# The masks of the causal heads' first bank and of half the banded blocks: from matrix products to VectorE, in a hybrid attention trunk

## The chip, the cores and the metric

The kernel runs on one core of a Trainium2 chip. A core has engines that run their own instruction streams and meet through semaphores: TensorE (PE, matrix products into PSUM banks of 128 x 512 f32), VectorE (DVE), ScalarE (ACT), GpSimd (POOL) and SyncE (SP), which here issues the transfers. The metric is the device time in microseconds. Three runs of the kernel before took 1720.56 to 1721.05 us, median 1720.91.

## The reference

Two layers, 512 tokens, width 1024. Each layer mixes three attention branches by gates and then has a squared-ReLU MLP. The change touches the masks of two of the branches:

```python
# branch A, 8 heads, causal, in blocks of 128 queries
s = jnp.where(key_pos[None, :] <= q_pos[:, None], s, -jnp.inf)
p = jax.nn.softmax(s, axis=-1).astype(v.dtype)
# branch B, 8 heads, sliding window of 128, so a block sees itself and the one before it
valid = (diff >= 0) & (diff < SWA_WINDOW)
s = jnp.where(valid[None, :, None, None], s, -jnp.inf)
m = jnp.maximum(jnp.max(s, axis=-1, keepdims=True), sink)
p = jnp.exp(s - m)
p = (p / (jnp.sum(p, axis=-1, keepdims=True) + jnp.exp(sink - m))).astype(v.dtype)
```

Branch C (stick-breaking, 8 heads) has a strict causal mask, which the kernel already applies behind its exponential; it is not touched.

## The kernel before

All matrix work is done in split precision: an operand is stored as a high part (fp32r, made by ACT as a copy) and a low part (the difference, made by DVE), and each product is three products: high by high, high by low, low by high. Weights come in chunks through a ring of four buffers; `split(c)` on ACT and on DVE makes the two parts of chunk c. Scores are kept transposed, keys on the partitions and queries along the columns, so that a softmax's maximum over keys goes across partitions.

A head of branch A (`CAUSAL`) has four key blocks, with 512, 384, 256 and 128 columns of queries that may see them, in three banks: bank 0 holds key block 0 (512 columns, its first 128 the diagonal block), bank 1 key blocks 1 and 3, bank 2 key block 2. A head of branch B (`BANDED`) has three key blocks of 256 columns (own block and next) and one of 128, in two banks; banded heads come in pairs. A mask is a matrix product: the identity by a constant that is -1e30 where the score is to go (`causal_mask`, and in `band_scores`). One head then goes through this chain:

- PE: `scores` (or `band_scores` for a pair), which adds the masks.
- DVE: `biggest`, four steps that fold the blocks into `mx` (512 columns). The first step of a causal head is a copy of bank 0; the first two of a banded head take the maximum with the sink (`floor`).
- GpSimd: the reduction of `mx` across partitions.
- PE: `less_biggest`, which subtracts it (`mla_shift`, `band_shift`).
- ACT: `soft_exp`, the exponential of each bank into `s_f` (1280 columns) or `bs_f` (896).
- ACT: `soft_hi`, the high part `p_hi`. DVE: `probs_lo`, the low part `p_lo`.
- PE: `values`. ACT: `soft_out`, 1/denominator through a logarithm and an exponential. DVE: `soft_out`, the product `of`, which frees the bank of the values.

Each engine's order is written out by hand. In the causal stage DVE's iteration h does: the maximum of head h+1, `mla_q` and `mla_qk` (splits of queries and keys for head h+2), `soft_out(h)`, a weight split, in the first layer's iterations 0 to 3 a part of the rotary angles (`angle_turns`, `angle_less`, `angle`, `angle_ahead`), `probs_lo(h+1)`, and the product of a gate tile (`scaled`), which frees the tile's bank. Projection tiles alternate between two banks, so each waits for the tile two before it. PE's iteration h does: scores of head h+1, `mla_q(h+2)` (with the keys for even heads), values of head h, and a gate tile with `mla_shift(h+1)` in its middle. In the banded stage DVE's iteration t, for the pair 2t and 2t+1, does two maxima, `mixed`, `soft_out`, `band_lo(2t)`, weight splits, `mixed`, `rope_turn` and `rope_in` or `stick_scaled`, then `band_den(2t)`, `band_lo(2t+1)`, `soft_out(2t)`. PE's does `band_values(2t-1)`, `out_tile` and `band_shift` twice, a tile, `band_values(2t)` and `band_scores(t+1)`. In the last pair `stick_scores(0)` follows `band_values(6)`, and waits for the last exponential of the banded heads. `soft_hi` of the odd head waits for the values of the even one.

## Time and profile before

| | |
|---|---|
| median of three runs | 1720.91 us |
| the profiled execution | 1720.57 us, span 1718.8 us |
| PE busy | 1693.2 us, 99% of the span |
| weight loads of PE | 1429.0 us, 83% |
| DVE busy | 1117.5 us, 65% |
| ACT busy | 852.8 us, 50% |
| GpSimd busy | 150.8 us, 9% |
| mean granted TensorE clock | 0.998 |
| chain that ended last | PE 83%, issue 6%, DVE 5%, ACT 3% |

Busy times are those of one profiled execution. Products overlap on PE, so a product's duration in the profile (0.39 us for 512 columns) is longer than the distance from its start to the start of the next; only distances between starts say what a product costs. An idle time of an engine stands in brackets in the timelines, with what released it; it costs only where something on the path waits for that engine. Times in the timelines are from the start of the span. The first layer's causal stage runs from about 51 to 154 us, its banded stage from about 160 to 244; in the second layer they lie some 850 us later.

### The profile page before, as it was taken

The numbers are of one execution on the slowest core, as the hardware profiler recorded it, in microseconds if no ns is written. First come the engines' busy times: TensorE is split into PE (matmuls) and PEld (weight loads), VectorE is DVE, ScalarE is ACT, GpSimd is POOL, SyncE is SP. The second block draws the span as 40 slices with busy tenths as digits, with TensorE's granted clock in tenths as the row PEclk, the third lists the DMA queues.
The fourth block names the chain that finished last, engine by engine and source line by source line (L and its number), as shares of the span: only waits on it lengthen the run. The fifth ranks groups of instructions, "written<-read, shape, count | busy, mean of one in ns | idle before, by whom it ended". The sixth has DMA issues, their size and how long they took to land.

```text
span 1718.8 us, 21730 instructions
## 1 busy us (share of the span) xinstructions
PE 1693.2 (99%) x8533; PEld 1429.0 (83%) x8533; DVE 1117.5 (65%) x1530; ACT 852.8 (50%) x1204; POOL 150.8 (9%) x142
## 2 busy tenths in 40 slices
PE   8999999999999999999999999999999999999997
PEld 6888888888898888888888888888888988888886
DVE  8887888886566534364597777888754765344545
ACT  7576566665455424131466755666644553231223
POOL 0111211111100000000001111111111000000000
PEclk9999999999999999999999999999999999999999
DMA  4121122222332222222321211122224222222222
GB/s 151 66 71 60 62 69 75 78 74 86 135 111 85 93 94 97 99 98 98 120 83 65 77 62 62 62 74 74 74 92 161 78 90 96 98 98 98 98 98 74
DMA packets 47495, 152.02 MB, mean 88 GB/s; under 512 B 5153, under 2 KB 9633, under 8 KB 47394
## 3 DMA queue, kind: packets, MB, share of 16 engines
q1 hardware_dynamic: 45664, 147.36, 24.7%
q10 hardware_dynamic: 1730, 3.28, 0.5%
q8 instruction: 68, 1.11, 0.3%
q14 instruction: 33, 0.27, 0.0%
HBM read 146.42 MB, written 4.19 MB: 88 GB/s over the span
## 4 chain that ended last, share of the span: by engine, by line
PE 83%; issue 6%; DVE 5%; ACT 3%; POOL 1%; DMA 1%; SPq 0%; DVEq 0%; POOLq 0%; ACTq 0%
PE bank L599 78%; PE bank L604 2%; PE bank L856 1%; PE bank L901 1%; POOL mix L2342 1%; ACT w_hi L1053 1%; DVE w_lo L1600 1%; POOL fb L2372 1%; PE bank L703 0%; DMA x<-in_x 0%; DVE hf L1647 0%; ACT dn L1110 0%; ACT dn L1108 0%; DVE h_lo L1635 0%; DVE of L1722 0%
## 5 line engine op out<-in xcount | busy, mean ns | idle before, releaser
L599 PE MATMUL bank<-h_hi,w_hi 128*128 128x512 f32 (+1 forms) x1224 | 477.3, 390 | 6.4 <-DVEq L1739 2.8
L599 PE MATMUL bank<-h_hi,w_lo 128*128 128x512 f32 (+1 forms) x1224 | 471.9, 386 | 0.0
L599 PE MATMUL bank<-h_lo,w_hi 128*128 128x512 f32 (+1 forms) x1224 | 471.6, 385 | 0.0
L1053 ACT ACTIVATE w_hi<-raw 128x1024 fp32r<-128x1024 f32 (+2 forms) x269 | 270.5, 1013 | 206.4 <-DMA raw<-in_w 205.9
L1600 DVE TENSOR_TENSOR w_lo<-raw,w_hi 128x1024 fp32r<-128x1024 f32 (+2 forms) x269 | 316.3, 1179 | 59.5 <-ACT w_hi L1053 52.7
L599 PEld LDWEIGHTS bank<-h_hi,w_hi 128*128 128x128 f32 x1224 | 230.1, 188 | 55.5 <-issue 6.2
L599 PEld LDWEIGHTS bank<-h_hi,w_lo 128*128 128x128 f32 x1224 | 229.9, 188 | 47.1
L599 PEld LDWEIGHTS bank<-h_lo,w_hi 128*128 128x128 f32 x1224 | 230.2, 188 | 44.8 <-issue 1.2
L599 PE MATMUL bank<-u_hi,w_hi 128*128 128x512 f32 (+1 forms) x560 | 208.0, 371 | 0.0
L599 PE MATMUL bank<-u_hi,w_lo 128*128 128x512 f32 (+1 forms) x560 | 207.7, 371 | 0.0
L599 PE MATMUL bank<-u_lo,w_hi 128*128 128x512 f32 (+1 forms) x560 | 207.7, 371 | 0.0
L599 PEld LDWEIGHTS bank<-u_hi,w_hi 128*128 128x128 f32 x560 | 105.5, 188 | 18.3
L599 PEld LDWEIGHTS bank<-u_lo,w_hi 128*128 128x128 f32 x560 | 105.5, 188 | 18.2
L599 PEld LDWEIGHTS bank<-u_hi,w_lo 128*128 128x128 f32 x560 | 105.5, 188 | 18.0
L1934 DVE TENSOR_TENSOR usq<-relu 128x512 f32<-128x512 f32 x64 | 44.2, 691 | 101.7 <-ACT relu L1258 101.2
L1258 ACT ACTIVATE relu<-bank 128x512 f32<-128x512 f32 x48 | 28.6, 595 | 136.5 <-PE bank L599 136.5
L1952 DVE TENSOR_TENSOR y<-bank,y 128x512 f32<-128x512 f32 x32 | 22.1, 691 | 98.7 <-PE bank L599 98.7
L599 PE MATMUL bank<-o_hi,w_hi 128*128 128x512 f32 x192 | 76.6, 399 | 0.0
L1260 ACT ACTIVATE u_hi<-relu 128x512 fp32r<-128x512 f32 x64 | 40.5, 633 | 70.1 <-DVE relu L1929 68.6
L599 PE MATMUL bank<-o_hi,w_lo 128*128 128x512 f32 x192 | 75.0, 390 | 0.0
L2342 POOL TENSOR_TENSOR mix<-mix,gate 128x512 f32<-128x512 f32 x32 | 44.4, 1390 | 346.5 <-DVE gate L1909 346.5
L599 PE MATMUL bank<-o_lo,w_hi 128*128 128x512 f32 x192 | 74.8, 390 | 0.0
(267 smaller groups left out, 2738.7 us busy)
## 6 DMA issues: line engine op xcount, KB each, us to landing
raw<-in_w SPq DMA_DIRECT2D x251, 512.0 KB, 3.2
x<-in_x SPq DMA_DIRECT2D x16, 256.0 KB, 3.5
side_raw<-in_w SPq DMA_DIRECT2D x6, 512.0 KB, 4.9
x_spill<-x ACTq DMA_DIRECT2D x8, 256.0 KB, 2.2
x<-x_spill SPq DMA_DIRECT2D x8, 256.0 KB, 3.0
out_y<-x SPq DMA_DIRECT2D x8, 256.0 KB, 2.1
raw<-in_w SPq DMA_DIRECT2D x8, 192.0 KB, 2.4
raw<-in_w SPq DMA_DIRECT2D x8, 128.0 KB, 2.3
```

The lines of the kernel that those rows point to most:

```text
L599: mm = pe.matmul(o, s, m, start=start and i == 0 and j == 0, stop=last and i == n - 1 and j == 2, skip_group_check=True)
L604: return pe.matmul(o, stationary, moving, start=False, stop=True, skip_group_check=True)
L856: return pe.matmul(to[:, off + col:off + col + w], a, m, start=(r, n, i) in STICK_STARTS, stop=i == 2, skip_group_check=True)
L901: mm = pe.matmul(pv_bank[:, q0:q0 + w], v[:, j, h % 2, :], part[:, s], start=i == 0 and part is p_hi, stop=part is p_lo, skip_group_check= ...
L1053: act.activation(chunk_in(gc, w_hi, side_hi)[:, 0:w], chunk_in(gc, raw, side_raw)[:, 0:w], ACT.Copy)\
L1258: act.activation(relu[:, n % 2, :], tile_bank(name)[:, :], ACT.Relu).then_inc(free_of(name), 1)
L1260: act.activation(u_hi[g % 2][:, t, :], relu[:, n % 2, :], ACT.Square).then_inc(u_h.sem, 1)
L1600: dve.tensor_tensor(chunk_in(gc, w_lo, side_lo)[:, 0:w], chunk_in(gc, raw, side_raw)[:, 0:w], chunk_in(gc, w_hi, side_hi)[:, 0:w].bitcast( ...
L1934: dve.tensor_tensor(usq[:, n % 2, :], relu[:, n % 2, :], relu[:, n % 2, :], ALU.mult)\
L1952: ins = dve.tensor_tensor(y[:, t, :], tile_bank(name)[:, :], y[:, t, :], ALU.add)
L2342: pool.tensor_tensor(mix[:, t, :], mix[:, t, :], gated_at(b, t), ALU.add).then_inc(mix_add.sem, 1)
L2372: pool.tensor_tensor(to, to, tri01[:, :], ALU.mult).then_inc(z_mask.sem, 1)
```

## The change

Constants gain two matrices, `BOUND`: 2^127 where a probability is kept and 0 where it is masked, for the diagonal and for the previous block. ACT copies them into a buffer `bound` in the setup.

Causal heads: bank 0 gets no mask product any more; banks 1 and 2 keep theirs. The first step of the maximum is now a sum of the first 128 columns and the mask constant, and a copy of the other 384. Behind the exponential DVE takes, in place, the minimum of `s_f`'s first 128 columns and `bound`.

Banded heads: in the first bank only the second half is masked by a product (256 columns instead of 512), in the second bank only the last 128 columns (the product of 256 goes). The first two steps of the maximum become (score max sink) + mask in one instruction. Behind the exponential DVE takes the minimum of two blocks of 256 columns and `bound`.

`soft_hi` on ACT waits for the new minimum (`probs_masked`).

```diff
@@ scores (PE)
-                        three(to[:, off + col:off + col + w], [(keys(j), queries(q0, w))], start=off + col == 0)
+                        mm = three(to[:, off + col:off + col + w], [(keys(j), queries(q0, w))], start=off + col == 0)
                         if n + 1 == len(pieces) or pieces[n + 1][3] != b:
-                            causal_mask(to, off, b, MASK_CAUSAL).then_inc(score_full.sem, 1)
+                            if b:
+                                mm = causal_mask(to, off, b, MASK_CAUSAL)
+                            mm.then_inc(score_full.sem, 1)
@@ band_scores (PE)
                                 if b == 0:
-                                    mm = add(band[r][0][:, :].rearrange("p (a c) -> p a c", a=2), cst[:, IDENT, :],
-                                             both.unsqueeze(1).broadcast_to([P, 2, 2 * P]))
+                                    mm = add(band[r][0][:, 2 * P:4 * P], cst[:, IDENT, :], both)
                                 else:
-                                    add(band[r][1][:, 0:2 * P], cst[:, IDENT, :], both)
                                     mm = add(band[r][1][:, 2 * P:3 * P], cst[:, IDENT, :], cst[:, MASK_CAUSAL, :])
@@ soft_hi (ACT)
                     act.wait_ge(*p_exp(banks_of(n + 1)))
+                    act.wait_ge(*p_mask(n + 1))
@@ setup (ACT)
+                act.activation(bound[:, :], cst_f[:, BOUND * P:(BOUND + 2) * P], ACT.Copy).then_inc(const_set, 1)
@@ biggest (DVE)
                         if banded and i < 2:
-                            ins = dve.tensor_scalar(to[:, q0:q0 + w], src, floor, None, ALU.max)
+                            both = cst[:, MASK_CAUSAL:MASK_PREV + 1, :].rearrange("p a c -> p (a c)").bitcast(F32)
+                            ins = dve.scalar_tensor_tensor(out=to[:, q0:q0 + w], in0=src, scalar=floor, in1=both,
+                                                           op0=ALU.max, op1=ALU.add)
                         elif i == 0:
-                            ins = dve.tensor_copy(to[:, q0:q0 + w], src)
+                            dve.wait_ge(const_set, 1)
+                            dve.tensor_tensor(to[:, 0:P], src[:, 0:P], cst[:, MASK_CAUSAL, :].bitcast(F32), ALU.add)
+                            ins = dve.tensor_copy(to[:, P:SEQ], src[:, P:SEQ])
@@ new (DVE)
+                def causal_masked(h):
+                    dve.wait_ge(const_set, 4)
+                    dve.wait_ge(*p_exp(banks_of(h) + 1))
+                    dve.tensor_tensor(s_f[:, 0:P], s_f[:, 0:P], bound[:, 0:P], ALU.min).then_inc(p_mask.sem, 1)
+
+                def band_masked(n):
+                    dve.wait_ge(*p_exp(banks_of(HEADS + n + 1)))
+                    halves = bs_f[n % 2][:, 0:6 * P].rearrange("p (a c) -> p a c", a=3)[:, 0:3:2, :]
+                    dve.tensor_tensor(halves, halves, bound[:, :].unsqueeze(1).broadcast_to([P, 2, 2 * P]), ALU.min)\
+                       .then_inc(p_mask.sem, 1)
@@ order of DVE
                     for j in range(NB - 1):
                         mla_v(j)
+                    causal_masked(0)
                     split(C["gate", 0, 2] + 2)
@@ in the loop over causal heads, behind the angles
                         if h + 1 < HEADS:
+                            causal_masked(h + 1)
                             probs_lo(h + 1, s_f[:, :], p_hi[:, :], p_lo[:, :])
@@ in the loop over banded pairs
                             soft_out(HEADS + n - 1)
+                        band_masked(n)
                         band_lo(n)
...
                             stick_scaled(0, t - 1)
+                        band_masked(n + 1)
                         band_den(n)
                         band_lo(n + 1)
```

DVE's order in the first layer's causal stage, from the split of head 3's queries to head 4's maximum (`tt` are the angles, `mix` the gate). Before:

```order
L1600 TENSOR_TENSOR w_lo<-raw,w_hi 128x1024
L1578 SCALAR_TENSOR_TENSOR tt_151<-tt_152,tt_151 128x512 x2
L1582 TENSOR_SCALAR tab<-tt_151 128x512
L1690 TENSOR_TENSOR p_lo<-s_f,p_hi 128x1280
L1682 TENSOR_TENSOR mix<-bank,rstd_x 128x512
L1711 CAST mx<-bank 128x512
L1713 TENSOR_TENSOR mx<-bank,mx 128x384
```

And with the change:

```order
L1604 TENSOR_TENSOR w_lo<-raw,w_hi 128x1024
L1582 SCALAR_TENSOR_TENSOR tt_152<-tt_153,tt_152 128x512 x2
L1586 TENSOR_SCALAR tab<-tt_152 128x512
L1727 TENSOR_TENSOR s_f<-s_f,bound 128x128
L1694 TENSOR_TENSOR p_lo<-s_f,p_hi 128x1280
L1686 TENSOR_TENSOR mix<-bank,rstd_x 128x512
L1718 TENSOR_TENSOR mx<-bank,cst 128x128
L1719 CAST mx<-bank 128x384
L1721 TENSOR_TENSOR mx<-bank,mx 128x384
```

The minimum stands behind the angles and ahead of the low part, and the copy is in two. PE's order at the end of `band_scores`, the second bank (masks are `bank<-cst`, key block 3's scores `128x128`), and the first product of `band_values`. Before:

```order
L828 MATMUL bank<-wq_hi,wk_hi 128x128 x2
L828 MATMUL bank<-wq_lo,wk_hi 128x128 x2
L828 MATMUL bank<-wq_hi,wk_lo 128x128 x2
L604 MATMUL bank<-cst 128x256
L604 MATMUL bank<-cst 128x128
L604 MATMUL bank<-cst 128x256
L604 MATMUL bank<-cst 128x128
L599 MATMUL bank<-bp_hi,wv_hi 128x256
```

And with the change:

```order
L832 MATMUL bank<-wq_hi,wk_hi 128x128 x2
L832 MATMUL bank<-wq_lo,wk_hi 128x128 x2
L832 MATMUL bank<-wq_hi,wk_lo 128x128 x2
L606 MATMUL bank<-cst 128x128 x2
L601 MATMUL bank<-bp_hi,wv_hi 128x256
L601 MATMUL bank<-bp_lo,wv_hi 128x256
```

Two products of 256 columns are gone there, and the two of 512 further ahead have 256. DVE's order in a banded pair, around the denominator of its even head. Before:

```order
L1793 TENSOR_TENSOR wq_lo<-ra,wq_hi 128x512
L1776 SCALAR_TENSOR_TENSOR rp_lo<-bank,rp_hi 128x512
L1781 SCALAR_TENSOR_TENSOR ra<-bank,cf 128x512
L1803 TENSOR_TENSOR dn<-bank,dn 64x512
L1690 TENSOR_TENSOR bp_lo<-bs_f_123,bp_hi 128x896
L1722 TENSOR_TENSOR of<-bank,dn 64x512
```

And with the change:

```order
L1812 TENSOR_TENSOR wq_lo<-ra,wq_hi 128x512
L1795 SCALAR_TENSOR_TENSOR rp_lo<-bank,rp_hi 128x512
L1800 SCALAR_TENSOR_TENSOR ra<-bank,cf 128x512
L1732 TENSOR_TENSOR bs_f_124<-bs_f_124,bound 128x2x256
L1822 TENSOR_TENSOR dn<-bank,dn 64x512
L1694 TENSOR_TENSOR bp_lo<-bs_f_124,bp_hi 128x896
L1741 TENSOR_TENSOR of<-bank,dn 64x512
```

The odd head's minimum stands between the rotation's product and the denominator.

## Rows read from the trace of the kernel before

**Rows 1.** The page, busy time of two engines and share of the span.
```profile
PE 1693.2 (99%) x8533; PEld 1429.0 (83%) x8533; DVE 1117.5 (65%) x1530; ACT 852.8 (50%) x1204; POOL 150.8 (9%) x142
```

**Rows 2.** Waits of PE: engine line waited for: us, times, longest us.
```profile
PE bank L599 <- DVEq L1739: 2.8, 2, 1.4
PE bank L599 <- DVE of L1722: 1.9, 6, 0.5
```

**Rows 3.** Groups by form (busy us, mean ns | idle before, us): mask products of PE.
```profile
L604 PE MATMUL bank<-cst 128*128 128x128 f32 x48 | 10.7, 222 | 0.0
L604 PE MATMUL bank<-cst 128*128 128x256 f32 x32 | 10.2, 345 | 0.0
L604 PE MATMUL bank<-cst 128*128 128x512 f32 x16 | 5.9, 448 | 0.0
```

**Rows 4.** Timeline of PE (start us, us, engine line op), the first head.
```profile
52.01 0.22 PE L604 MATMUL bank<-cst 128*128 128x128 f32 x1
52.07 0.39 PE L599 MATMUL bank<-mq_hi,mk_hi 128*128 128x384 f32 x1
```

**Rows 5.** Groups by form: steps of the causal maximum on DVE.
```profile
L1711 DVE CAST mx<-bank 128x512 fp32r<-128x512 f32 x16 | 10.9, 682 | 0.1
L1713 DVE TENSOR_TENSOR mx<-bank,mx 128x128 fp32r<-128x128 f32 x16 | 4.7, 292 | 1.7
```

**Rows 6.** Timeline of DVE, causal heads of the first layer.
```profile
75.85 1.49 DVE L1690 TENSOR_TENSOR p_lo<-s_f,p_hi 128x1280 fp32r<-128x1280 f32 x1 [0.21 <-ACT p_hi L1144]
87.29 1.49 DVE L1690 TENSOR_TENSOR p_lo<-s_f,p_hi 128x1280 fp32r<-128x1280 f32 x1 [0.54 <-ACT p_hi L1144]
99.21 0.43 DVE L1582 TENSOR_SCALAR tab<-tt 128x512 f32<-128x512 f32 x1
99.78 1.49 DVE L1690 TENSOR_TENSOR p_lo<-s_f,p_hi 128x1280 fp32r<-128x1280 f32 x1
113.13 0.69 DVE L1682 TENSOR_TENSOR mix<-bank,rstd_x 128x512 f32<-128x512 f32 x1
123.58 1.49 DVE L1690 TENSOR_TENSOR p_lo<-s_f,p_hi 128x1280 fp32r<-128x1280 f32 x1 [1.41 <-ACT p_hi L1144]
```

**Rows 7.** Timeline of ACT, head 3 of the first layer.
```profile
98.26 1.27 ACT L1144 ACTIVATE p_hi<-s_f 128x1280 fp32r<-128x1280 f32 x1
```

**Rows 8.** Timeline of PE: a key product, and the subtraction of head 7.
```profile
115.04 0.40 PE L599 MATMUL bank<-ckn_hi,w_hi 128*128 128x512 f32 x1
142.91 0.50 PE L604 MATMUL bank<-mxr,cst 128*128 128x512 f32 x1 [0.42 <-POOL mxr L2354]
```

**Rows 9.** Timeline of DVE, head 3 of the second layer.
```profile
949.56 1.49 DVE L1690 TENSOR_TENSOR p_lo<-s_f,p_hi 128x1280 fp32r<-128x1280 f32 x1 [1.79 <-ACT p_hi L1144]
```

**Rows 10.** Timeline of DVE, first pair of banded heads.
```profile
184.83 0.68 DVE L1781 SCALAR_TENSOR_TENSOR ra<-bank,cf 128x512 f32<-128x512 f32 x1
185.54 0.69 DVE L1803 TENSOR_TENSOR dn<-bank,dn 64x512 f32<-64x512 f32 x1
```

**Rows 11.** Timeline of ACT, the same place.
```profile
185.01 0.96 ACT L1144 ACTIVATE bp_hi<-bs_f 128x896 fp32r<-128x896 f32 x1 [0.82 <-PE bank L599]
186.27 0.63 ACT L1108 ACTIVATE dn<-dn 64x512 f32<-64x512 f32 x1 [0.30 <-DVE dn L1803]
```

**Rows 12.** Timeline of PE, the same place.
```profile
188.43 0.36 PE L599 MATMUL bank<-bp_hi,wv_hi 128*128 128x256 f32 x1 [0.51 <-DVE of L1722]
```

**Rows 13.** Timeline of DVE, ACT and PE, last pair of banded heads.
```profile
231.20 0.69 DVE L1722 TENSOR_TENSOR of<-bank,dn 64x512 f32<-64x512 f32 x1
231.36 0.95 ACT L1144 ACTIVATE bp_hi<-bs_f 128x896 fp32r<-128x896 f32 x1
234.64 0.57 ACT L1137 ACTIVATE bs_f<-bank 128x512 f32<-128x512 f32 x1
233.51 0.36 PE L599 MATMUL bank<-bp_hi,wv_hi 128*128 128x256 f32 x1
235.73 0.46 PE L856 MATMUL bank<-sb_hi 64*128 64x512 f32 x2 [0.62 <-ACT bs_f L1137]
```

More of the change, by code:

```diff
@@ L124 @@
 VECS = V_SINK + HEADS
-IDENT, SWAP, NEG_TRI, NEG_ONE, ONE, MASK_CAUSAL, MASK_PREV, NEG_PART, TRI_MOST = range(9)
-N_CONST = 9 * P
+IDENT, SWAP, NEG_TRI, NEG_ONE, ONE, MASK_CAUSAL, MASK_PREV, NEG_PART, TRI_MOST, BOUND = range(10)
+N_CONST = 11 * P
 TRIG = 4 * 4
@@ L282, in trunk @@
         at[0] += 24576
+        bound = place("bound", [P, 2 * P], F32)
         s_f = place("s_f", [P, CAUSAL_COLS], F32, r3)
@@ L404, in trunk @@
         mx_step = signal("max_step", 64)
+        p_mask = signal("probs_masked", 16)
         mx_all = signal("max_all", 16)
@@ L2386, in constants @@
     mats = [p == c, swap == c, -(p >= c).astype(np.float32), -np.ones((P, P)), np.ones((P, P)),
-            -BIG * (p > c), -BIG * (p <= c), np.full((P, P), -1.0 / P), MOST * (p < c)]
+            -BIG * (p > c), -BIG * (p <= c), np.full((P, P), -1.0 / P), MOST * (p < c),
+            MOST * (p <= c), MOST * (p > c)]
     const = np.concatenate([np.asarray(m, np.float32) for m in mats], axis=1)
```

## The prediction

> **What bounds the kernel now.** I read the page first: PE is busy 99% of the span, DVE 65% [rows 1]. So the end moves by what PE is spared and by what PE must newly wait for, and by nothing else. The second view is the list of PE's waits: they are few and small, and two of them lie in the stretches that the change touches, behind `mla_q`'s product on DVE and behind the banded heads' output product on DVE [rows 2]. The third view is the timeline around the masks, engine by engine, since what decides is how late each head's chain (maximum, GpSimd's reduction, subtraction, exponential, high part, low part, values) runs against PE's arrival at its next step. The reader is to see there who waits for whom: in the causal heads of the first layer DVE comes to `p_lo` at the moment at which ACT has the high part ready, or after it; in the second layer DVE stands idle for it.
>
> **What PE is spared.** Each causal head loses one mask product of 128 columns; the next product starts 0.06 us after it [rows 4]. That is 16 x 0.06 = 1.0. Each pair of banded heads loses two of 256 columns and has two of 512 halved; by the 0.06 for 128 columns that is 0.24 + 0.24, in 8 pairs 3.8. The counts stand in the groups: 16 of the 48, 16 of the 32, and the 16 of 512 [rows 3]. In all 4.8 us, if PE is what limits there. The lower bound of this gain is nothing, where PE then waits for a chain that does not depend on the mask.
>
> In the banded stage it is nothing. A pair's masks stand in `band_scores(t+1)`, between `band_values(2t)` and `band_values(2t+1)`, and PE waits in front of the latter for `of` from DVE [rows 12]. That chain starts at the end of `band_values(2t)` and does not see the masks, so PE only arrives earlier and waits longer. The first pair's masks stand ahead of `rotate(2)`, which waits for a split made from a tile that is older than they are. So of 4.8 only the causal 1.0 is left, half of it in each layer.
>
> **What DVE gets.** The maximum's first step, a copy of 512 columns at 0.68, becomes a sum of 128 and a copy of 384. The 128 column sum is like the 0.29 one of the same line group [rows 5], and two instructions overlap by their start; the two sizes give 0.39 / 384 = 1.0 ns a column and 0.16 fixed, of which about 0.08 overlaps the next one. So a head's maximum ends about 0.1 later (bounds: 0, and the whole 0.29). The banded first steps become three operand steps of the same 256 columns: I take no change (-0.05 to +0.1 each). The causal bound is 128 columns from SBUF: 0.29; the banded one 512 columns: 0.69, as every full tile step of DVE [rows 10]. ACT's extra copy of 256 columns in the setup is about 0.4, mostly in idle time of ACT: 0.1 on PE.
>
> What matters is the new wait: `p_hi` on ACT now waits for DVE's bound, so that the high part can no longer be made while DVE is busy with something else. Behind it on ACT stand `gate_soft`, or in the banded stage the next weight splits and the next head's exponentials.
>
> **Causal heads, first layer.** There DVE also computes the angles, in heads 0 to 3 of the loop, ahead of `p_lo` of heads 1 to 4. Head 3 shows it: DVE ends the angle at 99.64 [rows 6], ACT made the high part from 98.26 to 99.53 [rows 7], `p_lo` starts at 99.78. After the change DVE comes to the bound at 99.64, ends it at 99.93, ACT makes the high part in 1.27, and `p_lo` starts 1.6 after DVE's arrival (0.29 + 1.27 and two hand-overs). DVE, which had waited 0.1, waits 1.3 more and is late with all that follows; nearly back to back as it is here, it does not make that up. Per head: lateness + 0.1 (maximum) + 1.6 - the old wait. Head 0: 0.3. Head 1, old wait 0.2 [rows 6]: 1.8. Head 2, old wait 0.5 [rows 6]: 3.0. Head 3, 0.1: 4.6. Head 4, as head 3: 6.2. In head 5 DVE had waited 1.41 for the high part [rows 6] and its bound fits beside the exponentials of the other banks: 6.4. Head 6 adds 0.1 and 0.3: 6.8; head 7's maximum makes it 6.9.
>
> PE has slack of two microseconds at most in these heads, so it is soon drawn along. The key product of head 6 starts at 115.04 [rows 8] and takes the bank that the gate product freed at 113.82 [rows 6]; 6.2 later that is 120.0, and PE waits some 5. At head 7's subtraction PE had already waited 0.42 for GpSimd [rows 8], with no slack at all: there the whole 6.9 arrives. Bounds: if each high part costs only the bound's 0.3 the term is 2; if nothing of the old waits counts it is 8.5. I take 6.9, since the arrivals are in the rows.
>
> **Causal heads, second layer.** No angles: DVE waited 1.79 for the high part at head 3 [rows 9] and has as much at most others. The bound waits only for the first bank's exponential and is done about when the last one ends, so the chain grows by 0.0 to 0.2 a head. The slack takes it, but head 7's subtraction sees 0.3, against 0.5 spared on PE and 0.1 lost behind `mla_q`'s bank in front of `gate 0,2` [rows 2]. I take +0.1 (bounds -0.5 to +1).
>
> **Banded heads, each layer.** The odd head's bound stands behind `rope_in` or `stick_scaled` and ahead of `band_den`. In pair 0 DVE starts its step before at 184.83 [rows 10], so the bound runs from 185.44 to 186.13, and ACT's high part starts at 186.16, not at 185.01 [rows 11]; 0.30 of the 1.15 is idle time that ACT had before its logarithm [rows 11]. So `of`, and PE's `band_values(1)` [rows 12], come 0.85 later. Pair 1: the even head's bound makes DVE late by its own 0.7, its splits and rotation follow, and the odd bound stands in the way again: I take 0.7. Pair 2: DVE waited for PE before that place: 0. Pair 3: DVE is free at 231.81 (0.61 after 231.20 [rows 13]), the bound ends at 232.50, the high part starts 1.17 later than 231.36, and PE stood at `band_values(6)` and then at `stick_scores` without slack [rows 13], the latter for the exponential of head 7 that ACT issues behind it. So 1.2. Sum 2.8 a layer (bounds 1.2, if the first two are absorbed, and 4).
>
> **The sum.** 0.1 + 6.9 + 0.1 + 2 x 2.8 = 12.7 us. The profiled execution took 1720.57 beside its span of 1718.8: 1733.3. The median shown is 0.3 higher: 1733.6.
>
> **The rivals.** (A) PE is the bound and DVE has room. For it speaks PE's 99% against DVE's 65% [rows 1]. Then only the 4.8 count: 1720.9 - 4.8 = 1716.1. Against it: both stretches already show PE waiting for DVE [rows 2, 12], with no slack at head 7 [rows 8]. The Trainium skill (Perfetto Trace Analysis, "Identifying the Most-Contended Engine") says to find the engine with the highest occupancy and to optimize that one first. By that rule the change is the right one and gives 1716; the trace bears out the occupancy, not the conclusion, as the waits in rows 2 lie where the work is put. 0.07.
>
> (B) DVE's lateness in the first layer is made up, by waits that shrink when everything behind is late, and only the banded chains and a part of it count. It decides if head 7's subtraction is less than 2 late: 0.1 + 1.5 + 0.1 + 5.6 = 7.3, 1728.2. Against it: between heads 1 and 5 the waits on ACT that I saw are hand-overs that DVE itself starts. 0.15.
>
> (C) The lateness goes on: the gates and splits that DVE does in the sliding-window and stick-breaking stages come late too, and weights are not ready. PE would lose 6 more: 1740. Against it: from head 7 on PE is late by as much as DVE, and both have slack afterwards. 0.07.
>
> (D) The banded masks' gain is kept and the causal lateness is small: near 1720.9, within the 0.2% (3.4 us) that a measurement here can tell from no change. 0.04.
>
> **The chances.** The forecast 0.67. Slower by over 0.2% (above 1724.3): forecast, B and C, 0.89. Within: 0.04. Faster by over 0.2%: 0.07. The likeliest time is 1733.6; 8 times in 10 it lies between 1726 and 1738, which takes in B, and the bounds of the first layer's term only where one of the others goes the same way.
>
> **What would show it.** In the changed profile: `p_lo` of the first layer's heads 1 to 4 each with an idle time of about 1.3 before it, its bound just ahead; heads 1 to 7 of the second layer nearly as before; PE waiting on `gate` or `p_lo` of DVE in the first layer's heads 2, 3, 4 and 6, and at head 7's subtraction about 7 later than before against 0 to 0.2 in the second layer; a longer wait ahead of `band_values` of heads 1 and 3, and one of about 1.2 at head 6. It is wrong if the span from the start to head 7's subtraction grows by less than 4, or if the two layers grow alike there.

## The result: 18 us slower, and the profile after

The changed kernel takes 1739.0 us (median of 4 runs, 1737.87 to 1740.08) against 1720.98 us of the kernel before on the same chip (4 runs, 1720.56 to 1721.65): a ratio of 1.0105, 95% interval 1.0093 to 1.0117. The forecast was 1733.6 with a range of 1726 to 1738. The direction and most of the mechanisms were right; the time lies above the range. The four runs show a mean granted clock of TensorE of 0.993 to 0.995, where the profiled run of the kernel before has 0.998. One run of the banded half alone, a kernel that comes below, took 7634.74 us and is left out of its median.

The profiled execution took 1738.03 us, its span is 1736.2 us, 17.4 more than before. Its page, the row that answers [rows 1]:

```profile
PE 1695.5 (98%) x8501; PEld 1429.3 (82%) x8501; DVE 1133.9 (65%) x1578; ACT 852.6 (49%) x1205; POOL 150.8 (9%) x142
```

VectorE (DVE) has 48 instructions and 16.4 us more. TensorE (PE) has 32 instructions fewer and yet 2.3 us more of busy time, which is the first hint at what the forecast missed. The waits of PE from 40 to 1110 us (columns as in [rows 2]):

```profile
PE bank L601 <- DVE of L1741: 8.0, 6, 2.0
PE bank L601 <- DVE mix L1686: 3.8, 2, 2.4
PE bank L601 <- DVEq L1758: 3.1, 2, 1.6
PE bank L601 <- DVE bp_lo L1694: 2.6, 2, 1.4
PE bank L601 <- DVE p_lo L1694: 1.4, 2, 0.7
```

The wait for `of`, 1.9 in six times before [rows 2], is 8.0. Waits for `mix`, `p_lo` and `bp_lo` are new. Groups by form (busy us, mean ns | idle before), answering [rows 5]:

```profile
L1718 DVE TENSOR_TENSOR mx<-bank,cst 128x128 fp32r<-128x128 f32 x16 | 4.5, 283 | 0.1
L1719 DVE CAST mx<-bank 128x384 fp32r<-128x384 f32 x16 | 8.8, 549 | 0.0
L1714 DVE SCALAR_TENSOR_TENSOR bmx<-bank,vec_all,cst 128x256 fp32r<-128x256 f32 x32 | 15.4, 480 | 1.9
L1727 DVE TENSOR_TENSOR s_f<-s_f,bound 128x128 f32<-128x128 f32 x16 | 4.6, 285 | 0.5 <-DVE tab L1586 0.2 <-DVE tab L1595 0.2
L1732 DVE TENSOR_TENSOR bs_f<-bs_f,bound 128x512 f32<-128x512 f32 x16 | 12.0, 747 | 0.2
```

The single prices were as estimated (0.29 and 0.69; two of the banded minima took 1.17, which lifts their mean, see the end).

**Where the time lies.** The starts of the same TensorE instructions in both traces, how late the changed kernel is, and how late the forecast's sum has it there (us):

| place | before | after | late | by the sum |
|---|---|---|---|---|
| first scores | 51.24 | 50.77 | -0.5 | +0.1 |
| subtraction, head 3 | 96.38 | 97.96 | 1.6 | |
| subtraction, head 5 | 120.39 | 125.97 | 5.6 | |
| subtraction, head 7 | 142.91 | 149.73 | 6.8 | 7.0 |
| banded values, head 1 | 188.43 | 196.21 | 7.8 | 7.85 |
| banded subtraction, head 2 | 192.66 | 202.04 | 9.4 | 7.85 |
| banded values, head 3 | 207.08 | 217.14 | 10.1 | 8.6 |
| first stick scores | 235.73 | 247.36 | 11.6 | 9.8 |
| second layer, first scores | 901.22 | 912.84 | 11.6 | 9.8 |
| subtraction, head 7 | 992.33 | 1003.79 | 11.5 | 9.9 |
| banded values, head 1 | 1037.70 | 1050.30 | 12.6 | 10.7 |
| banded subtraction, head 4 | 1060.66 | 1076.97 | 16.3 | 11.4 |
| banded values, head 6 | 1082.80 | 1100.32 | 17.5 | 12.6 |

The causal half of the first layer did what was forecast, head by head: reckoned from the first scores, `p_lo` of heads 1 to 6 starts 1.8, 3.1, 4.9, 6.7, 7.0 and 7.2 late, where the forecast has 1.8, 3.0, 4.6, 6.2, 6.4 and 6.8. Head 3 on DVE and ACT, answering [rows 6, 7] (timeline: start us, us, engine line op, in brackets the idle time before it):

```profile
101.88 0.43 DVE L1586 TENSOR_SCALAR tab<-tt 128x512 f32<-128x512 f32 x1
102.52 0.29 DVE L1727 TENSOR_TENSOR s_f<-s_f,bound 128x128 f32<-128x128 f32 x1 [0.21 <-DVE tab L1586]
104.20 1.49 DVE L1694 TENSOR_TENSOR p_lo<-s_f,p_hi 128x1280 fp32r<-128x1280 f32 x1 [1.39 <-ACT p_hi L1147]
```

and the high part on ACT, in the same view:

```profile
102.90 1.27 ACT L1147 ACTIVATE p_hi<-s_f 128x1280 fp32r<-128x1280 f32 x1 [2.38 <-issue]
```

The high part no longer runs beside the angle: it starts behind the minimum, and `p_lo` waits 1.39 for it where it had waited 0.1; it does so in heads 1 to 7 of both layers, and in the second layer that is no longer than before (1.79 [rows 9]). On PE, the key product of head 6 (before without a wait) and the subtraction of head 7, answering [rows 8]:

```profile
120.12 0.51 PE L601 MATMUL bank<-ckn_hi,w_hi 128*128 128x512 f32 x1 [2.37 <-DVE mix L1686]
...
149.73 0.50 PE L606 MATMUL bank<-mxr,cst 128*128 128x512 f32 x1 [0.52 <-POOL mxr L2377]
```

PE waits 2.37 there and not the 5 of the forecast, because its earlier waits had already made it 2.7 late.

**What was not in the sum** stands between two rows of the table: from the banded values of head 1 to the next subtraction, PE computes without a wait and nothing was changed, yet it loses 1.6. The answer to [rows 12], and what comes behind it:

```profile
196.21 0.36 PE L601 MATMUL bank<-bp_hi,wv_hi 128*128 128x256 f32 x1 [1.92 <-DVE of L1741]
...
197.64 0.72 PE L601 MATMUL bank<-o_hi,w_hi 128*128 128x512 f32 x1
198.16 0.63 PE L601 MATMUL bank<-o_lo,w_hi 128*128 128x512 f32 x1
198.58 0.63 PE L601 MATMUL bank<-o_hi,w_lo 128*128 128x512 f32 x1
...
201.35 0.40 PE L601 MATMUL bank<-o_hi,w_hi 128*128 128x512 f32 x1
201.58 0.40 PE L601 MATMUL bank<-o_lo,w_hi 128*128 128x512 f32 x1
```

Products of 512 columns that start 0.23 apart start 0.43 apart for 3.4 us. The windows show why (stretch and its length, us; busy time of PE, its weight loads, DVE, ACT and GpSimd; then the granted clock PEclk, DMA share, GB/s), of after:

```profile
190.00:195.00 5.00, 4.30 (x42) 3.70 (x40) 4.12 (x6) 2.89 (x5) 0.00 (x0) 1.00 0.34 105
195.00:200.00 5.00, 3.79 (x18) 3.34 (x19) 4.18 (x10) 2.29 (x4) 1.78 (x1) 0.76 0.00 0
200.00:205.00 5.00, 5.00 (x23) 4.12 (x22) 2.70 (x5) 1.56 (x4) 1.78 (x1) 0.89 0.00 0
1050.00:1055.00 5.00, 4.70 (x20) 4.22 (x21) 3.84 (x9) 1.44 (x3) 1.78 (x1) 0.66 0.01 2
1070.00:1075.00 5.00, 3.80 (x16) 3.58 (x17) 4.18 (x9) 1.52 (x3) 1.35 (x1) 0.66 0.00 0
```

and of before in the same part of the program:

```profile
188.00:193.00 5.00, 4.58 (x27) 4.10 (x28) 4.30 (x11) 1.57 (x3) 1.78 (x1) 1.00 0.00 0
193.00:198.00 5.00, 5.00 (x26) 4.17 (x25) 4.09 (x6) 4.81 (x8) 1.78 (x1) 1.00 0.17 57
1037.00:1042.00 5.00, 4.49 (x27) 3.86 (x27) 4.30 (x10) 1.84 (x3) 1.78 (x1) 1.00 0.01 3
```

Three times, behind the values of head 1 in both layers and of head 3 in the second, the granted clock is at its lower level (1.2 instead of 2.4 GHz, 0.5 in this scale) for 3.4 us. I call such a stretch a spell. Each costs 1.5 to 1.6 us, 4.65 in all, and each stands behind a wait of PE that the change has made longer: 1.92 above against 0.51 [rows 12], and in the second layer

```profile
1050.30 0.36 PE L601 MATMUL bank<-bp_hi,wv_hi 128*128 128x256 f32 x1 [1.95 <-DVE of L1741]
...
1071.20 0.35 PE L601 MATMUL bank<-bp_hi,wv_hi 128*128 128x256 f32 x1 [1.36 <-DVE of L1741]
```

Before had no spell in its two banded stages. Its only one stands at the very end, where TensorE has run out of products:

```profile
1710.00:1715.00 5.00, 0.00 (x0) 0.00 (x0) 4.86 (x10) 0.00 (x0) 0.00 (x0) 0.73 0.39 137
```

That the waits caused the spells is at this point a theory.

### The profile page after: what moved, and what is told of

It reads as the page before. It is cut to its first block, busy times and chain, and to the rows that moved or that the text cites. A ratio compares the mean times of both kernels' runs of the same rounds, so it can differ in the third digit from the quotient of the medians.

```text
span 1736.2 us, 21733 instructions
## 1 busy us (share of the span) xinstructions
PE 1695.5 (98%) x8501; PEld 1429.3 (82%) x8501; DVE 1133.9 (65%) x1578; ACT 852.6 (49%) x1205; POOL 150.8 (9%) x142
## 4 chain that ended last, share of the span: by engine, by line
PE 72%; issue 8%; DVE 7%; ACT 4%; POOL 1%; DMA 0%; DVEq 0%; POOLq 0%; ACTq 0%
PE bank L601 68%; PE bank L606 2%; ACT w_hi L1055 1%; PE bank L858 1%; DVE w_lo L1604 1%; PE bank L903 1%; POOL mix L2365 1%; POOL fb L2395 1%; DVE bmx L1714 0%; PE bank L705 0%; DVE ra L1810 0%; DVE hf L1651 0%; ACT dn L1112 0%; ACT dn L1110 0%; ACT bp_hi L1147 0%
```

## The experiments

The theories: (1) the causal half costs by the wait of ScalarE (ACT) for a minimum that stands behind the angle; (2) the banded half costs by its place in DVE's order; (3) what the forecast lacked is TensorE's clock, which falls because PE idles longer. The rival to 3: DVE's added 16 us come through by themselves, and the clock goes with them. A kernel's time below is its median over its timed runs, its ratio is against before on the same chip; a trace shows one of these runs; "late" is always the start of a TensorE instruction against the same one before.

**The causal half alone** (the banded masks and maximum as before).

```
-                        band_masked(n)
...
-                        band_masked(n + 1)
...
+                    if n < HEADS:
+                        act.wait_ge(*p_mask(n + 1))
```


> The causal part of the change alone; the banded heads are masked by PE as before. Theory (a new wait of ACT's high part for DVE, which in the first layer stands behind the angles): head 7's subtraction in the first layer comes about 6.8 us later than before, as in the changed kernel (142.91 to 149.73), the second layer's causal stage gives nothing or 0.2 back, the total is 1720.9 + 6.3 to 6.9, about 1727.5, and the clock stays at the upper level. Rival (DVE's added work as such, spread evenly): both causal stages lengthen alike, each by about 3.

1729.02 us, ratio 1.0046 (1.0030 to 1.0062). From the first scores to head 7 it loses 7.5 (-0.8 to +6.7), in the second layer 0.2. That is the theory's share; the expectation that the clock stays up failed, as it had a spell of its own, behind the key product that had waited as in the full change:

```profile
115.00:120.00 5.00, 2.65 (x16) 2.03 (x15) 3.33 (x7) 3.66 (x5) 0.00 (x0) 1.00 0.23 93
120.00:125.00 5.00, 5.00 (x20) 4.42 (x20) 3.96 (x8) 2.41 (x5) 1.78 (x1) 0.66 0.31 105
```

It made PE later by 1.2 at head 5 and hardly at head 7 (7.5 against 7.3 in the full change), since that subtraction waits for DVE's maximum anyway. The full change had the same wait of 2.37 and no spell behind it.

**The banded half alone.**

```
-                    causal_masked(0)
...
-                            causal_masked(h + 1)
...
+                    if n >= HEADS:
+                        act.wait_ge(*p_mask(n + 1 - HEADS))
```


> The banded part of the change alone; the causal heads are masked by PE as before. Theory: the three waits per layer (about 0.95, 0.7, 0 and 1.45 for the four pairs, 6.2 in all) and beside them spells in which TensorE's granted clock is at 1.2 GHz, each costing about 1.55 (three of them in the profiled execution of the changed kernel): 1720.9 + 6.2 + 4.6 = 1731.7, with at least two such spells in the profile. Rival (no clock term, the rest of the changed kernel's loss is somewhere else in it): 1727.1 and no spell.

1732.12 us (1731.12, 1732.12 and 1735.32), ratio 1.0073 (1.0051 to 1.0094). The trace shows 0.98 at pair 0, 0.67 at pair 1, 0 at pair 2 and 1.3 at pair 3, the same in both layers, and three spells that cost 1.4 to 1.6 each: two in the first layer, one in the second. So the banded half, not the causal one, is the larger, and the spells come with it. They are not at the same places as in the full change.

**The causal minimum ahead of the angle steps**, with the rest as in the causal half alone.

```
+                        if h + 1 < HEADS:
+                            causal_masked(h + 1)
                         if now[0] == 0:
...
-                            causal_masked(h + 1)
```


> As the causal part alone, but DVE does the bound of head h+1 ahead of the angle steps of iteration h instead of behind them. Theory: ACT makes the high part while DVE computes angles, as before the change; the first layer's lateness is gone, head 7's subtraction comes between 0.5 earlier and 1.5 later than before, the total is 1720 to 1722.5. Rival (DVE's added work as such): no better than the causal part alone, about 1727.5.

1721.87 us, ratio 1.0007 (0.9997 to 1.0016). The same instructions in another order are 7.1 us faster. Head 3 on DVE:

```profile
98.07 0.28 DVE L1728 TENSOR_TENSOR s_f<-s_f,bound 128x128 f32<-128x128 f32 x1
98.27 1.41 DVE L1585 SCALAR_TENSOR_TENSOR tt<-tt,tt 128x512 f32<-128x512 f32 x2
99.72 0.43 DVE L1589 TENSOR_SCALAR tab<-tt 128x512 f32<-128x512 f32 x1
100.29 1.49 DVE L1697 TENSOR_TENSOR p_lo<-s_f,p_hi 128x1280 fp32r<-128x1280 f32 x1
```

`p_lo` no longer waits: ACT's high part runs beside the angle again. That settles theory 1. Up to head 4 each head even gains 0.12, then DVE's added time shows at heads 5 and 7 (0.5 and 1.4).

**The minimum without the wait**: before, with the 16 causal minima written to a tile that nobody reads; masks and maximum as before. The edit, against before:

```
+                    dve.tensor_tensor(scratch[:, :], s_f[:, 0:P], bound[:, 0:P], ALU.min).then_inc(p_mask.sem, 1)
...
+                    causal_masked(0)
...
+                            causal_masked(h + 1)
```


> The kernel before with one thing added: DVE takes the minimum of the first 128 columns of the probabilities and the bound at the same 16 places as in the causal part of the change, but writes it to a buffer of its own that nobody reads, and ACT does not wait. PE's masks and the maximum are as before. Theory (the wait is what costs, not the instruction): DVE is late by 0.2 a head in the first layer, about 1.0 at head 7's subtraction, total 1721.5 to 1722.5. Rival (DVE's added instruction costs): nearly the causal part's full loss, 1726 or more.

1721.55 us, ratio 1.0005 (0.9995 to 1.0014): DVE's time by itself costs 0.8 at head 7, and in the whole kernel nothing that a measurement can tell. The wait is the price.

**Banded half, with TensorE's banded masks kept as well.**

```
+                                    mm = add(band[r][0][:, :].rearrange("p (a c) -> p a c", a=2), cst[:, IDENT, :],
+                                             both.unsqueeze(1).broadcast_to([P, 2, 2 * P]))
...
+                                    add(band[r][1][:, 0:2 * P], cst[:, IDENT, :], both)
```


> The banded half of the change alone (VectorE's sum in the maximum's step and its minimum behind the exponential), but TensorE's products with the banded masks of both heads of a pair are kept as well, so the masks are added twice (a masked score is then twice as low, the rest as before). It adds 0.11 us of TensorE's work per head to the kernel with the banded half alone, and takes nothing from VectorE. Theory (the missing 4.65 us of the change are TensorE's granted clock, which fell to 0.5 behind the lengthened idles of TensorE before the banded values of heads 1 and 3): VectorE's chain is the same, so the waits' own 6 to 6.5 us stay; the idles get 0.1 to 0.2 us shorter, which decides at most one of the spells: 1727 to 1733. If a spell of 3.4 us at 0.5 stands in the trace, it costs 1.4 to 1.6 us at its place. Rival (TensorE's columns count, so the masks' products have a price on the path): 0.2 us in each pair more than the banded half alone, 1733.7 + 1.6 = 1735.

1730.21 us, ratio 1.0054 (1.0039 to 1.0069), as expected: with more work not slower than the banded half alone. Pairs 0, 1 and 3 cost 0.99, 0.67 and 1.3 as there, so the masks that the change takes from TensorE are worth nothing in this stage, as the forecast said. Three spells stand in its profile too, behind idles of 1.66, 1.61 and 1.35 (here and below an idle of PE is reckoned from the end of the columns of the product before, which is about 0.2 more than the bracket shows). It leans to theory 3 and does not decide it.

**Banded half, the odd head's minimum earlier.**

```
                         mixed(n + 1)
+                        band_masked(n + 1)
                         if t < 2:
...
-                        band_masked(n + 1)
                         band_den(n)
```


> The banded half alone, with the minimum of the odd head issued ahead of the turn of the next projection (rope_turn) and of the scaling of the stick's queries, and so ahead of the denominators of the even head, in the place right behind the odd head's mixing. Theory: what made the banded part dear is where the odd head's minimum stood in VectorE's order, and through it the wait of TensorE before the odd head's values; with the minimum earlier the odd head's terms (0.95 and 0.68 us in pairs 0 and 1) fall to 0.2 us or nothing, and with them the idles behind which the granted clock fell, so no spell at 0.5: left are pair 3's 1.3 to 1.5 us in each layer: 1723 to 1725. Rival 1 (the price is VectorE's work whatever its order: 16 more minima and no slack): 1731 to 1733.7 as with the banded half alone. Rival 2 (the clock's spells come from the work saved on TensorE and not from the idles): pairs 0 and 1 cost nothing, but two or three spells of 1.5 us stay, 1727 to 1729.

1734.01 us, ratio 1.0078 (1.0062 to 1.0093): this expectation failed. Pair 0 fell only to 0.68, pair 1 rose to 1.14, and four spells stand in the profile. The reader sees the reason in what PE waits for at the values of heads 1 and 3:

```profile
188.49 0.36 PE L601 MATMUL bank<-bp_hi,wv_hi 128*128 128x256 f32 x1 [1.66 <-DVE of L1739]
...
208.30 0.36 PE L601 MATMUL bank<-bp_hi,wv_hi 128*128 128x256 f32 x1 [1.83 <-DVE of L1739]
```

It is `of` of the even head, which waits for that head's denominators `dn`. The minimum stood ahead of `dn` in both orders and makes it 0.69 late in both; in pair 1 it now also delays `tmp` (the scaled queries of the next branch), whose copy stands ahead of the high part in ACT's queue, so that `bp_lo` waits for it 0.81 instead of 0.34. Theory 2 as I had put it (the place behind the turn) was wrong; its chain goes through `dn`. The four timed runs show the clock's part plainly: 1731.25 and 1732.18 at a mean granted clock of 0.994, 1735.84 and 1736.93 at 0.991, for the same program.

**Banded half, TensorE's idles filled.** 14, 9 and 3 superfluous mask products ahead of the score signals of pairs 1 to 3.

```
+FILL = (0, 14, 9, 3)
...
+                            if b and t:
+                                for _ in range(FILL[t]):
+                                    mm = add(band[1][1][:, 0:2 * P], cst[:, IDENT, :], both)
                             mm.then_inc(score_full.sem, 2)
```


> The banded half alone, with 14, 9 and 3 more mask products of 256 columns (each repeats a mask on scores that are masked anyway) ahead of the score signal of pairs 1, 2 and 3: work that nobody needs, put where TensorE would wait for the values of the odd head of the pair before. It adds 26 x 0.11 = 2.9 us of TensorE's work to each layer. Theory (the granted clock fell behind the idles): with the idles filled the clock stays at 1.00, and a kernel with 5.7 us more work is 4 to 5 us faster than the banded half alone, 1727 to 1730 (up to 1731 if the scores signalled later delay the maximum). Rival (the lost time is VectorE's, the clock follows it and costs nothing by itself): the same 1733.7, or later by what the fillings delay, 1735 to 1739.

1726.12 us, ratio 1.0034 (1.0021 to 1.0047): some 5.7 us of useless work more (by the 0.11 us that a product of 256 columns costs), and 6.0 us faster than the banded half alone, where I expected 4 to 5. The filling and what it leaves of the wait, in the timeline of PE:

```profile
186.24 2.16 PE L607 MATMUL bank<-cst 128*128 128x128 f32 x16
188.62 0.36 PE L602 MATMUL bank<-bp_hi,wv_hi 128*128 128x256 f32 x1 [0.23 <-DVE of L1743]
```

The windows behind it, in the columns used above:

```profile
190.00:195.00 5.00, 5.00 (x26) 4.17 (x26) 4.46 (x9) 2.25 (x4) 3.55 (x2) 1.00 0.00 0
...
235.00:240.00 5.00, 3.72 (x25) 3.61 (x27) 4.97 (x7) 3.71 (x7) 0.00 (x0) 0.79 0.31 107
1045.00:1050.00 5.00, 5.00 (x26) 4.14 (x25) 3.67 (x7) 3.11 (x6) 2.90 (x2) 1.00 0.00 0
```

The values of head 1 start as late as without the filling (1.0 from the first scores), so the filling took nothing from DVE's chain. But the clock stays up behind them; the banded half alone had 0.66 at 190 to 195. One spell is left, at 238, behind pair 3, where nothing is filled. The terms of the pairs are those of the banded half alone (0.98, 0.68, 0 and 1.3 in the first layer). Between the two profiled runs (1732.12 and 1727.18) the banded stages make 2.7 us of the difference, about what two spells fewer are worth, and 2.2 lie ahead of the first scores, in scatter. The other timed runs speak for the clock as well: all five of this kernel have 0.997 or 0.998, the three of the banded half alone 0.992 to 0.995, and none of the five is as slow as the fastest of the three. This shows theory 3: take the idle away, leave DVE's work and what waits for it, and the time of the spells is gone.

**Both minima early, the whole change.**

```
+                        if h + 1 < HEADS:
+                            causal_masked(h + 1)
...
-                            causal_masked(h + 1)
...
                         mixed(n + 1)
+                        band_masked(n + 1)
...
-                        band_masked(n + 1)
```


> The whole change with both minima earlier: the causal one ahead of the angle steps, the odd banded one right behind the odd head's mixing. Theory: the causal half costs about 1 us (as it did by itself in this place) and the banded half 3 us (pair 3), with no spell of TensorE's clock at 0.5 in the banded part: 1723 to 1726. Rival (the parts depend on each other, or VectorE's 16 us of added work come through elsewhere once both are there): over 1728.

1734.72 us, ratio 1.0079 (1.0062 to 1.0096): outside what I expected, for the reason just given. The causal part is as cheap as by itself (1.4 up to head 7, -0.2 in the second layer), while the banded stages cost 9.1 and 7.7, of which 6.0 and 4.6 are spells: all six idles of 1.3 to 2.1 before the values of heads 1, 3 and 6 have one, the first of them twice as long as the others.

```profile
190.00:195.00 5.00, 4.74 (x17) 4.38 (x18) 3.37 (x9) 1.28 (x3) 1.78 (x1) 0.50 0.00 0
195.00:200.00 5.00, 5.00 (x21) 4.04 (x21) 2.78 (x5) 1.21 (x4) 1.78 (x1) 0.83 0.00 0
...
215.00:220.00 5.00, 5.00 (x20) 4.11 (x21) 3.59 (x9) 1.90 (x4) 3.53 (x2) 0.78 0.00 0
```

**The banded minimum without the wait**, the counterpart of the causal one: before, plus 16 minima of 510 columns into an unread tile. The edit, against before:

```
+                    dve.tensor_tensor(scratch[:, :, :], halves,
...
+                                      [:, 0:2 * P - 1].unsqueeze(1).broadcast_to([P, 2, 2 * P - 1]), ALU.min)\
+                       .then_inc(p_mask.sem, 1)
```


> The kernel before with the sixteen banded minima added to VectorE at their places, but into a tile that nobody reads (510 columns instead of 512), without ScalarE waiting for them; masks by TensorE and the maximum's first step as before. So only VectorE's time is added. Theory (in pairs 0 and 1 the price is the minimum's 0.69 us ahead of the denominators dn in VectorE's order, through dn and of to the bank of the odd head's values; pair 3's price is the wait of bp_hi for the minimum): pairs 0 and 1 cost 0.6 to 0.7 us each as in the banded half with the masks kept, pair 3 0 to 0.5: 2.4 to 3.8 us for both layers, and TensorE's idles before the odd heads' values get to 1.2 to 1.5 us, behind which one or two spells of the granted clock at 0.5 may come (1.5 us each): 1723 to 1727. Rival (the price is ScalarE's wait for the minimum): 1720.5 to 1722, all pairs below 0.3 us.

1721.98 us, ratio 1.0009 (1.0000 to 1.0018), less than I expected. Only pair 0 is late, by 0.6 in each layer, through `dn`:

```profile
185.46 0.68 DVE L1725 TENSOR_TENSOR scratch<-bs_f,cst 128x510 f32<-128x510 f32 x1
186.17 0.69 DVE L1817 TENSOR_TENSOR dn<-bank,dn 64x512 f32<-64x512 f32 x1
...
188.22 0.68 DVE L1736 TENSOR_TENSOR of<-bank,dn 64x512 f32<-64x512 f32 x1 [0.23 <-ACT dn L1113]
```

Pairs 1 and 3 cost nothing, so their 0.67 and 1.3 are the wait of ACT, and so is 0.35 of pair 0. No spell stands in this profile, with PE idle for 1.27 at the place. Of the ten timed runs five have a mean clock of 0.998 and five 0.996, the two slowest (1723.89, 1724.44) among the latter; whether a spell stood in these, no trace shows.

**The whole change, TensorE's idles filled.** The filling above, in the changed kernel.

> The whole change, with 14, 9 and 3 more mask products of 256 columns (each repeats a mask on scores that are masked anyway) ahead of the score signal of pairs 1, 2 and 3, as in the banded half with filled idles: 5.7 us more of TensorE's work. Theory: the fillings cost no time, and the spells of the granted clock behind the odd heads' values go, which were what the forecast's sum lacked: 1739.0 less 3 to 5 spells of 1.55 us: 1731 to 1734.5, round the forecast's own 1733.6; spells behind pair 3's idle, which is not filled, may stay. Rival (the clock is no cause of its own, or falls elsewhere instead): 1737 or more.

1735.68 us, ratio 1.0086 (1.0072 to 1.0100): 3.3 us faster than the changed kernel with 5.7 us of work more. That is between what I expected (1731 to 1734.5) and the rival (1737 or more), and so bears theory 3 out in direction and only in part in size. The spells behind the values of heads 1 and 3 are gone in both layers:

```profile
195.00:200.00 5.00, 4.80 (x39) 4.38 (x36) 4.08 (x8) 2.33 (x4) 0.61 (x1) 1.00 0.00 0
200.00:205.00 5.00, 5.00 (x25) 4.17 (x24) 3.71 (x8) 3.05 (x5) 2.96 (x2) 1.00 0.00 0
...
245.00:250.00 5.00, 4.39 (x32) 4.28 (x34) 4.62 (x7) 3.68 (x7) 0.00 (x0) 0.74 0.15 55
...
1055.00:1060.00 5.00, 5.00 (x27) 4.24 (x26) 3.60 (x7) 3.13 (x7) 2.37 (x2) 1.00 0.00 0
```

In the profiled execution one spell stands behind pair 3 at 247, where PE still idles 1.6, one behind the key product at 121 and one in the setup, and its first scores were 0.7 late instead of 0.5 early. In the second layer pair 1 costs 1.0, where it costs 0.7 without the filling. The four timed runs (1734.53 to 1736.78) differ by 2.2 us at clocks of 0.995 to 0.997, and two with the same 0.997 differ as much, so the clock does not explain all of it.

**A version meant to beat both**: the early causal minimum only for heads 0 to 3 of the first layer and 0 to 6 of the second.

```
+ON_DVE = (4, 7)
+        def on_dve(n):
+            return n < ON_DVE[now[0]]
```


> The causal half with its minima ahead of the angle steps, but only for heads 0 to 3 of the first layer and 0 to 6 of the second; the others have their masks from TensorE as before. In the version with all heads TensorE's landmarks came 0.12 us earlier with each head up to head 4 and then lost 0.5 us at head 5 and 1.3 us up to head 7 of the first layer, and 0.3 us at head 7 of the second. Theory: those losses go, and 0.8 to 1.1 us are gained on the kernel before: 1719.4 to 1720.1, a ratio of 0.9995, which is within what a measurement can tell. Rival (the losses follow whatever head is the last with a minimum): as with all heads, 1721 to 1722.

1721.54 us, ratio 1.0004 (0.9995 to 1.0013): no gain, and not the 1719.4 to 1720.1 that I expected. The 0.12 a head are there (-0.42 at the first scores, -0.72 at head 3), then 0.8 is lost up to the subtraction of head 7, though heads 4 to 7 have no minimum; why, no run shows. No version that I tried beats the kernel before.

## Why the prediction was off

**Right.** The direction, and the reason for it: PE's 4.8 us were not to be had where PE waits for DVE. The causal term of the first layer was 6.9; measured from the first scores it is 7.3, and the causal half alone gives 7.5. The moved minimum and the one without a wait show that its mechanism was the right one too. The second layer's causal term was +0.1, measured -0.15. Pair 0 was 0.85, measured 0.95 and 1.0; pair 1 was 0.7, measured 0.68; pair 2 was 0, measured 0. In pair 0 the forecast saw one of two paths: beside ACT's late high part the minimum also makes the denominators `dn` late on DVE, and that path alone gives 0.6 when nothing waits for the minimum. In pair 1 its reason is only half right: the 0.7 does not come from DVE's added time, which costs nothing there, but from the wait that ACT now has in both heads of the pair.

**Mis-sized.** Pair 3 was 1.2; it measured 1.57 and 1.33. A causal mask product was taken at 0.06, the distance to the product behind it; that product's own distance to the next then falls from 0.23 to 0.18, and TensorE gains 0.12 a head where it waits for nobody (11.73 late at head 1 of the second layer, 11.13 at head 6). The head start of the setup went the other way (-0.5 instead of +0.1), but the kernels' first scores stand anywhere from 0.9 early to 1.3 late, and the four kernels with the banded half that share one setup (alone, masks kept, early minimum, filled) cover that whole range, so it is scatter between executions.

**The step that failed is the sum**, 0.1 + 6.9 + 0.1 + 2 x 2.8: it took every wait of PE at its own length and let PE go on at full clock behind it. In the profile three spells at 1.2 GHz add 4.65. With them and the 0.6 of the banded terms, the 0.4 of the causal one, and -0.85 from the setup and the second layer, 12.7 becomes 17.5, which is what the last row of the table has; without them the sum would have been right to 0.2 us, in part because the other errors cancel. The forecast said for pair 0 that `band_values(1)` comes 0.85 later and added PE's earlier arrival as lost; it did not ask what a wait that so grows from 0.51 [rows 12] to 1.92 does to the engine. Both experiments with filled idles bear this out in time: 6.0 us in the banded half, 3.3 in the whole.

The Trainium skill has a cause of this kind (TensorE: Matmul & The Clock Gate, "HAM oscillation — how this bites in real kernels"): it describes a kernel whose TensorE falls back to the slow clock because it waits for transfers between tiles. The trace agrees in kind, with 0.66 to 0.76 in the windows behind the waits; the waits of that kernel are longer than these, and that idles as short as 1.3 to 2.2 us can be followed by a spell is what the traces of this case show, not that section. The forecast did not weigh the clock at all. The trace of before, with its clock at 1.00 in the windows of the banded stage, gave no hint of it there; that the clock can fall stands only at its end.

**The rivals.** A (PE is the bound) fell: only the second layer's causal stage gains, and 0.15. B (made up) fell: head 7 is 6.8 late, not under 2. C named a time near the result, 1740, but is wrong: between the first stick scores and the second layer's first scores the lateness stays at 11.6, so nothing goes on behind the banded stage. Its nearness is chance. D (a small causal lateness) fell with B.

**The range** took its upper end from the bounds of the terms in the sum. A cost that depends on the sum's waits themselves was in none of them.

## What to carry to other kernels

A new wait of TensorE is priced at its length plus what the clock loses behind it: here an idle of 1.3 to 2.2 us in the banded stage carried a further 1.5 us in 21 of 32 cases. When a step is handed from a busy engine to an idler one, look where the receiver's step falls in its order, and put it ahead of work that can run beside what waits for it: the causal half cost 8.3 us in one place and 1.2 in the other. An engine's 65% share says nothing of a wait in a chain.

## What the runs showed that was not expected

- The granted clock falls behind idles of TensorE far shorter than its low spells. In the traces of the seven kernels with the banded half, PE idled 32 times for 1.3 to 2.2 us before the banded values (start of the product less the end of the columns before it), and behind 21 of them a spell stood: 3.4 us long (in one case twice that), 1.5 us lost. None stood behind the idles of 1.1 and less. Which of them are hit seems to change from one execution to the next: runs of one program are 5 us apart, the slower ones at a lower mean clock (0.991 against 0.994).
- The same idle elsewhere is not punished: PE idles 1.6 to 2.1 before the products at 57 and 907 us of before in all 13 kernels, and none of these 26 idles has a spell behind it. Behind the wait of 2.4 for the key product one stands in two of three kernels. What differs (the half-size products around the banded values, perhaps) was not tested and stays open.
- Superfluous products can pay: 5.7 us of them saved 6.0 us.
- A minimum of 512 columns that ran wholly beside GpSimd's reduction took 1.17 us instead of 0.69, once in each layer. The timeline of DVE and then of POOL (GpSimd):

```profile
182.29 1.17 DVE L1732 TENSOR_TENSOR bs_f<-bs_f,bound 128x512 f32<-128x512 f32 x1
```

and beside it

```profile
181.87 1.78 POOL L2354 PARTITION_ALL_REDUCE bmxr<-bmx  x1 [5.88 <-DVE bmx L1721]
```

The chain behind it had slack. The traces show more of it: `ra<-ra,rb`, also 512 columns, takes 1.05 instead of 0.69 where it runs inside a reduction (at 167.94 before, 174.74 after), and it and the minimum end at the same point, 1.59 after the reduction's start, though they begin 0.54 and 0.42 into it. `o_lo<-of,o_hi`, which begins 1.0 into one (at 148.91), takes 0.68. It looks as if such an instruction is held up in the first part of a reduction and not in the rest; no run tests it.
